# A fused transformer block on one core: the first projection on raw, transposed rows, and four smaller moves

## What is computed

```python
def rmsnorm(x, g):
    y = x * lax.rsqrt(jnp.mean(x * x, axis=-1, keepdims=True) + RMS_EPS)
    return y * g

def hybrid_mixer(h, w_in, ...):                  # h = rmsnorm(x, norm_mix)
    proj = h @ w_in
    (fq, fk, fv, f_logit, nq, kc, vc, ksl, vsl, kwn, vwn,
     nsa_gate_logit, merge_logit) = split_columns(proj, IN_SPLITS)
    ... fox attention on fq, fk, fv; NSA attention on nq with three sets of keys,
    ... rotary turning of nq, ksl, kwn
    g = jax.nn.sigmoid(merge_logit)
    up = jnp.einsum('bsnc,ncd->bsnd', ys, w_branch)
    return jnp.sum(g * up, axis=2) @ w_out

def attention_mixer(h, ...):       # second block: 16 meta tokens ahead of the 256
    ... banded attention with sinks; every query sees the meta tokens too

def deltanet_mixer(h, norm_w, w_in, ...):
    u = rms_norm(h, norm_w) @ w_in
    qkv, z, b, a = jnp.split(u, ...)
    ... causal convolution on qkv, delta rule
    return (rms_norm(o, o_norm_w) * jax.nn.silu(z)) @ w_out

def second_block(x, ...):
    ... return h[:, N_META:]       # the meta rows are dropped at the end
```

## Time and profile before

| | |
|---|---|
| median of 3 runs | 1620.73 us (1619.58 to 1621.23) |
| the profiled execution, its own time | 1621.65 us |
| its span | 1619.6 us |
| TensorE busy | 1584.4 us, 98% of the span |
| VectorE busy | 1164.3 us, 72% |
| ScalarE busy | 904.2 us, 56% |
| GpSimd busy | 105.4 us, 7% |

### The profile page before, as it was taken

The page is one execution under the profiler, slowest core; times in us unless marked ns, Lnnn a source line. Parts: engine busy times, 40 slices in busy tenths (PEclk is TensorE's granted clock), DMA queues, the critical chain, the costliest instruction groups (busy, mean ns, idle before and its releaser), DMA issues. The chain is left out here.

```text
span 1619.6 us, 33683 instructions
## 1 busy us (share of the span) xinstructions
PE 1584.4 (98%) x12906; PEld 1422.1 (88%) x12906; DVE 1164.3 (72%) x1987; ACT 904.2 (56%) x1605; POOL 105.4 (7%) x78
## 2 busy tenths in 40 slices
PE   7999999999999999999999999999999999999998
PEld 6888988999999999998888888878777889988877
DVE  5678666798988999986666666667655658755565
ACT  4357753455556767766666666654565645344443
POOL 0000000200000000000000000006001333200000
PEclk9999999999999999999999999999899999999999
DMA  6642355566555444446666666643233445300014
GB/s 219 185 155 81 114 169 157 170 183 181 182 181 157 143 132 138 131 137 208 194 192 191 192 191 194 194 151 119 65 91 94 152 146 159 128 3 3 3 41 143
DMA packets 63076, 229.56 MB, mean 142 GB/s; under 512 B 7008, under 2 KB 7264, under 8 KB 62960
## 3 DMA queue, kind: packets, MB, share of 16 engines
q1 hardware_dynamic: 62960, 227.94, 45.9%
HBM read 226.86 MB, written 1.05 MB: 141 GB/s over the span
## 5 line engine op out<-in xcount | busy, mean ns | idle before, releaser
L1161 DVE TENSOR_TENSOR tile_low<-weights,tile_high 128x1024 fp32r<-128x1024 f32 x252 | 308.0, 1222 | 131.2 <-ACT tile_high L1151 131.0
L1151 ACT ACTIVATE tile_high<-weights 128x1024 fp32r<-128x1024 f32 x252 | 268.1, 1064 | 134.1 <-issue 134.1
L182 ACT ACTIVATE tile_high<-weights 128x1024 fp32r<-128x1024 f32 x168 | 177.4, 1058 | 213.5 <-issue 58.6
L1233 PE MATMUL banks<-parts,tile_high 128*128 128x256 f32 x2048 | 270.5, 285 | 0.3 <-PEq L3129 0.3
L194 DVE TENSOR_TENSOR tile_low<-weights,tile_high 128x1024 fp32r<-128x1024 f32 x145 | 178.0, 1229 | 122.0 <-ACT tile_high L182 109.7
L1233 PEld LDWEIGHTS banks<-parts,tile_high 128*128 128x128 f32 x2048 | 254.1, 191 | 0.9 <-issue 0.9
L1562 PE MATMUL banks<-tile_high,parts 128*128 128x512 f32 x1024 | 253.0, 389 | 0.9 <-ACT parts L1520 0.9
L1562 PEld LDWEIGHTS banks<-tile_high,parts 128*128 128x128 f32 x1024 | 192.1, 188 | 40.9 <-issue 1.1
L236 PE MATMUL banks<-parts,tile_high 128*128 128x272 f32 (+1 forms) x1136 | 156.8, 290 | 0.8 <-ACT big L323 0.8
L236 PEld LDWEIGHTS banks<-parts,tile_high 128*128 128x128 f32 x1136 | 145.5, 188 | 9.6 <-issue 7.5
L1238 PE MATMUL banks<-parts,tile_low 128*128 128x256 f32 x1024 | 143.7, 283 | 1.0 <-DVE tile_low L1161 1.0
(11 more groups left out here) (417 smaller groups left out, 2221.8 us busy)
## 6 DMA issues: line engine op xcount, KB each, us to landing
weights<-in_peer_u SPq DMA_DIRECT2D x128, 512.0 KB, 3.5
weights<-in_peer_v SPq DMA_DIRECT2D x128, 512.0 KB, 3.5
weights<-in_dn_in SPq DMA_DIRECT2D x49, 512.0 KB, 3.5
weights<-in_in_t SPq DMA_DIRECT2D x19, 512.0 KB, 3.5
weights<-in_attn_t SPq DMA_DIRECT2D x18, 512.0 KB, 3.5
weights<-in_in_m SPq DMA_DIRECT2D x16, 512.0 KB, 3.5
weights<-in_wq SPq DMA_DIRECT2D x16, 512.0 KB, 3.6
weights<-in_dn_out SPq DMA_DIRECT2D x16, 512.0 KB, 3.6
```

Source lines behind the costliest of these rows:

```text
L182: k.nc.scalar.activation(k.high[:, m % 2, :], k.ring.view(n), ACT.Copy).then_inc(*k.high_made.up())
L1151: k.nc.scalar.activation(k.high[:, (s + j) % 2, :], k.ring.buf[:, j % RING, :], ACT.Copy).then_inc(k.high_made.sem, 1)
L1161: k.nc.vector.tensor_tensor(k.low[:, (s + j) % 2, :], k.ring.buf[:, j % RING, :], k.high[:, (s + j) % 2, :].bitcast(F32), ALU.subtract).th ...
L1233: ins = nc.tensor.matmul(ps[:, bank, 0:S], high[:, c, :], x[:, c, :], start=part + c == 0, stop=False)
```

## The change

- **The first projection takes rows that are not normalised.** The host also passes `x` transposed (`xt`). ScalarE and VectorE split `xt * norm_mix` directly; the diagonal matmuls are gone. The root is worked out while the first three tiles run; two matmuls with a matrix of ones then spread its reciprocal over all partitions (`root_row`). Every sum of the projection is multiplied by it on VectorE, the values at their copy, and the 16 merge gates by GpSimd in `attention_stage`. The sigmoid of the gates waits for these.
- **The keys are projected once**: 17 tiles, not 19. VectorE writes the turned keys to both halves of the partitions.
- **In `prepare_stage`** TensorE runs three sixths of the first merge tile ahead of the gates' transposes, not five.
- **The steps of the meta tokens' attention** stand at units 1, 3, 4, 6 and 8; the first two instructions are a step of their own.
- **The `z` tiles** are projected for the 256 tokens alone.

```diff
+def input_projection(k, into, prefetch, following):
...
+        @block.sync
+        def _(sp):
+            sp.dma_start(k.param[:, :], k.dram["param"]).then_inc(*k.param_landed.up(16))
+            for half in range(2):
+                sp.dma_start(columns[:, 4 * half:4 * half + 4, :],
+                             k.dram["xt"][:, 4 * half:4 * half + 4, :]).then_inc(*k.columns_landed[half].up(16))
+            load_tiles(sp, k, 3)
+            for tt in range(NT):
+                sp.dma_start(k.h[:, tt, :], k.dram["x"][:, tt, :]).then_inc(*k.x_landed[tt].up(16))
+            sp.dma_start(k.common[:, :], k.dram["const_common"]).then_inc(*k.common_landed.up(16))
+            load_tiles(sp, k, 10)
...
+        @block.scalar
...
+            for c in range(KC):
+                act.wait_ge(*k.columns_landed[c // 4].at(16))
+                nc.scalar.activation(high[:, c, :], columns[:, c, :], ACT.Copy,
+                                     scale=weight[:, c:c + 1]).then_inc(*parted.up())
+            for n in range(3):
+                make_high(act, k, n)
+            for tt in range(NT):
+                act.wait_ge(*k.x_landed[tt].at(16))
+                nc.scalar.activation(scratch[:, tt, :], k.h[:, tt, :], ACT.Square,
+                                     accum_out=sums[:, tt:tt + 1]).then_inc(*summed.up())
+            act.wait_ge(*chain.at(1))
+            nc.scalar.activation(root, y, ACT.Sqrt).then_inc(*rooted.up())
+            for n in range(3, IN_TILES):
+                make_high(act, k, n)
...
+        @block.vector
...
+            def take(i):
+                dve.wait_ge(k.ring.used.sem, i + 1)
+                sum_halves(k, into(i), ps[:, i % 8, :]).then_inc(*halves.up())
+                dve.wait_ge(*halves.last())
+                nc.vector.tensor_tensor(into(i), into(i), k.root_row, ALU.mult).then_inc(*taken.up())
...
+            for n in range(4, IN_TILES):
+                make_low(dve, k, n)
+                upto = n - 1 if n > 5 else n - 2
+                for i in range(done, upto):
+                    take(i)
+                done = upto
...
+        @block.tensor
+        def _(pe):
+            for i in range(IN_TILES):
+                if i == 3:
+                    pe.wait_ge(*cleared.at(2))
+                    pe.wait_ge(*scaled.at(NT))
+                    for tt in range(NT):
+                        ins = nc.tensor.matmul(ps[:, spread_bank, tt * P:tt * P + P], ones, diagonal(tt),
+                                               start=True, stop=True)
+                    ins.then_inc(*spread.up())
...
+                tile_both(pe, k, i, ps[:, i % 8, :], S, {"left": left} if i == 0 else None)
...
-            merged(0, 0, 5)
+            merged(0, 0, 3)
...
-            swap(NQ)
+            swap(T[:, NQ:NQ + 4, :], 4)
...
-            merged(0, 5, 6)
+            merged(0, 3, 6)
...
-            swap(KSL)
+            swap(k.raw_keys, 2)
...
+        @block.gpsimd
+        def _(pool):
+            for i in range(N_MERGE):
+                pool.wait_ge(gated.sem, i + 1)
+                nc.gpsimd.tensor_tensor(k.T[:, MERGE + i, :], k.T[:, MERGE + i, :], k.root_row,
+                                        ALU.mult).then_inc(*scaled_gates.up())
...
                 if c % 4 == 2:
+                    act.wait_ge(*gates_scaled.at(N_MERGE))
                     part = gate[:, :, 4 * (c // 4):4 * (c // 4) + 4, :]
                     nc.scalar.activation(part, part, ACT.Sigmoid).then_inc(*opened.up())
...
-            meta_steps = (1, 2, 4, 6)
+            meta_steps = (1, 3, 4, 6, 8)
...
-                if u == 1:
+                if u == 2:
                     make_low(dve, k, gate_tile(1))
...
             for u in range(len(units) + 1):
-                if u == 2:
-                    meta["scalar"](act)
                 if u < len(units):
                     exps(u)
+                if u == 3:
+                    meta["scalar"](act)
...
-    psum = lambda kind, i: ps[:, bank[kind](i), 0:L]
+    psum = lambda kind, i: ps[:, bank[kind](i), 0:S if kind == "z" else L]
+    tokens = lambda kind: slice(META if kind == "z" else 0, L)
```

More of the change, by code:

```diff
@@ L323, in merge_gate, with norm_programs @@
     k.nc.scalar.activation(k.T[:, MERGE + i, :], src, ACT.Copy).then_inc(*gated.up())
-def norm_programs(k, tiles, weight, cols, following, halves=True, scaled_rows=False, fetch=()):
+def norm_programs(k, tiles, weight, cols, following, scaled_rows=False, fetch=()):
     nc, ps = k.nc, k.ps
@@ L341, in norm_programs @@
     diagonal = lambda i: scratch[0:tiles[i][1], i, 0:tiles[i][1]]
-    ahead = range(k.tiles[following] + (1 if halves else 0), k.tiles[following] + AHEAD)
+    ahead = range(k.tiles[following] + 1, k.tiles[following] + AHEAD)
     def sync(sp):
-        if not halves:
-            fetch_inputs(sp, k)
         for dst, src in fetch:
@@ L351, in scalar @@
     def scalar(act):
-        if not halves:
-            act.wait_ge(*cleared.at(1))
-            nc.scalar.activation(k.norms[:, 47:48], k.norms[:, 47:48], ACT.Sqrt).then_inc(*loaded.up())
-            for i, (h, rows) in enumerate(tiles):
-                act.wait_ge(*k.x_landed[i].at(16))
-                nc.scalar.activation(scratch[0:rows, i, :], h, ACT.Square,
-                                     accum_out=sums[0:rows, i:i + 1]).then_inc(*summed.up())
-        act.wait_ge(*chain.at(3 if scaled_rows else 2 if halves else 1))
+        act.wait_ge(*chain.at(3 if scaled_rows else 2))
         nc.scalar.activation(root, y, ACT.Sqrt).then_inc(*rooted.up())
@@ L362, in scalar @@
             make_high(act, k, m)
-        if not halves:
-            act.wait_ge(*k.param_landed.at(16))
         for c in range(KC):
@@ L378, in vector @@
         else:
-            if not halves:
-                nc.vector.memset(k.norms[:, 47:48], 1.0).then_inc(*cleared.up())
-            if halves:
-                done(nc.vector.tensor_tensor(sums, sums, k.norms[:, 40:40 + n], ALU.add))
-            else:
-                dve.wait_ge(*summed.at(t))
+            done(nc.vector.tensor_tensor(sums, sums, k.norms[:, 40:40 + n], ALU.add))
             done(nc.vector.tensor_scalar(y, sums, 1.0 / D, EPS, ALU.mult, ALU.add))
@@ L387, in vector @@
         newton(nc, dve, chain, y, root, inv, step)
-        if not halves:
-            dve.wait_ge(*k.common_landed.at(16))
         for i, (h, rows) in enumerate(tiles):
@@ L394, in vector @@
             make_low(dve, k, m)
-        if not halves:
-            dve.wait_ge(*k.param_landed.at(16))
         for c in range(KC):
@@ L406, in product @@
                                     start=True, stop=True)
-        if halves:
-            keep_busy(k, 7, 3)
+        keep_busy(k, 7, 3)
         if t > NT:
@@ L568, in turn_rows, with turn_queries, turn_both_keys @@
         dve.wait_ge(*vec.last())
+    def turn_queries(dve):
+        x, y = T[:, NQ:NQ + 4, :], T[:, KSL:KSL + 4, :]
+        turned_part(dve, 0, x, y, 4)
         nc.vector.tensor_tensor(x, x, y, ALU.add).then_inc(*vec.up())
+        dve.wait_ge(*vec.last())
+    def turn_both_keys(dve):
+        x, y = k.raw_keys, rot[:, 0:2, :]
+        turned_part(dve, 1, x, y, 2)
+        for g in range(2):
+            mine = slice(HD * g, HD * g + HD)
+            for half in range(2):
+                nc.vector.tensor_tensor(T[HD * half:HD * half + HD, KSL + g:KSL + g + 3:2, :], x[mine], y[mine],
+                                        ALU.add).then_inc(*vec.up())
         dve.wait_ge(*vec.last())
@@ L2219, in _ @@
                     pe.wait_ge(*taken.at(i - 1))
-                tile_T(pe, k, first + t, psum(kind, i), lambda c: (high[:, c, :], low[:, c, :]),
+                of = tokens(kind)
+                tile_T(pe, k, first + t, psum(kind, i), lambda c: (high[:, c, of], low[:, c, of]),
                        norm=norm if t == 0 else None)
@@ L3179, in first_block @@
     k.x_landed = k.start("x_landed_0", "x_landed_1")
+    k.columns_landed = k.start("columns_landed_0", "columns_landed_1")
     k.common_landed, k.param_landed, k.const_landed = k.start("common_landed", "param_landed",
                                                                           "const_first_landed")
[L3182 removed]
     with k.joined():
[L3185 to L3187 removed]
+        k.raw_keys = k.rot[:, 2:4, :]
+        into = lambda i: k.raw_keys[:, i - KSL, :] if KSL <= i < KSL + 2 else k.T[:, i if i < KSL else MISC, :]
+        input_projection(k, into, k.tiles["in_fv"] + RING, "in_fv")
         def copy(dst, banks):
```

126 lines of the change are left out of this document (85 added, 41 removed).

## The result

| | before | after |
|---|---|---|
| median, 5 runs of each on one chip | 1621.23 us (1619.58 to 1624.73) | 1608.76 us (1606.69 to 1611.55) |
| ratio of the times | | 0.9922, 95% interval 0.9905 to 0.9938 |
| the profiled execution, its own time | 1621.65 us | 1609.04 us |
| its span | 1619.6 us | 1607.1 us |

In a later comparison, beside other kernels, the changed kernel took 1607.34 us against 1619.45 (ratio 0.9922, 0.9909 to 0.9935). The forecast was 1608.4 us: the sum came out, but not every term of it.

The account below looks back on a forecast made before the run. TensorE, busy 98% of the span, was taken to bound the kernel. The terms sum to -12.3 us; from the profiled 1621.65, less 0.92 to reach the median, this gives 1608.4 us, range 1603.5 to 1615.

Parts of the forecast that it names:

- start: First projection: tile 0 starts at 10.5 us, not 16.06, but at half clock; -2.2 us, between -3.9 and -1.2.
- the root's product per sum: First projection: VectorE's extra 0.43 us multiplication per tile stays hidden under TensorE's 2.82; 0 us.
- keys once: First projection: TensorE runs two tiles fewer; -5.6 us.
- `prepare_stage`: This stage: a 0.8 us wait for the gates' sigmoid against a cheaper keys' permutation; +0.2 us, from -0.9 to +1.1.
- gates on GpSimd: First attention: GpSimd's 13 multiplications hold up VectorE, about 0.1 us a unit reaching TensorE; +1.2 us, from 0 to +4.
- second block's attention: Shifted meta steps remove most of a 1.91 us wait and the half clock behind it; -4.0 us, from -1.6 to -5.3.
- z: Projection of z on 256 tokens, not 272: 16 tiles each 0.12 us shorter; -1.9 us.
- the ring: Weight slots shift with two tiles fewer; sub-keys land at 288.0 us, before their use at 288.73; 0 us, up to +3.
- Rival 1: Second block's attention: the clock still falls, so the part brings only 1.6 us; total 1610.8 us, chance 0.20.
- Rivals 2, 3 and 4: GpSimd's lock reaches TensorE every unit, 1616.3 us (0.10); start brings nothing, 1611.1 (0.10); GpSimd multiplication costs 2.39 us, 1638.3 (0.02).

Follow-up runs that it names:

- the first edit: Changed kernel with the meta tokens' steps back at units 1, 2, 4 and 6 and gate tile 1's split at unit 1: median 1611.89 us.
- the two edits: Changed kernel with the meta tokens' steps at their old places, 1611.89 us; kernel before with only the new places, 1616.76 us against 1621.69.

## Why the prediction was right, point by point

| term | forecast | in the first pair of traces | what the experiments add |
|---|---|---|---|
| start | -2.2 | -2.72 | cold start 1.3 to 2.8, mean 2.1 |
| the root's product per sum | 0 | 0 | |
| keys once | -5.6 | -5.51 | not undone, read from the traces alone |
| `prepare_stage` | +0.2 | +2.40 | +1.3 to +2.4 in five traces, -0.85 without its three waits |
| gates on GpSimd | +1.2 | 0 | 0 with none, under 0.7 with two |
| second block's attention | -4.0 | -5.25 | 5.0 by undoing it, 4.9 by adding it |
| z | -1.9 | -3.24 | 3.25 by undoing it |
| the ring | 0 | 0 | |
| not in the sum: half clock at 1080 us | | +1.62 | in 6 of 12 traces |
| small steps elsewhere | | +0.20 | |
| sum | -12.3 | -12.50 | |

- **Start.** TensorE began at 11.10 and not at 10.5, since the rows landed at 6.80 and not at 5.7; later traces have 9.72 to 10.74, so 10.5 was a fair middle. The half clock cost 1.97 us in tile 0, where I had 2.9 from half of 5.9; the 2.9 is just past the upper end of what nine traces show. The two errors went against each other. The root took the room that I had given it: diagonals at 20.0, tile 2's end at 21.4.
- **`prepare_stage`** is the step that failed, by 2.2 us, and twice the bound of +1.1 that I had given. Five traces have this order and no half clock inside the stage; they take 23.13 to 24.26 us against 21.86, so the error is 1.1 to 2.2. The wait for the sigmoid was 1.43 and not 0.8, since I took the second merge tile's landing, which ScalarE waits for ahead of it, from the trace of before, and it came 0.65 us later against the stage's start. The second wait, 0.44, is this kind of landing again. The third, 1.11, I had denied: "VectorE's work on the keys stays alike (four additions on half the partitions for one on all)". An addition of 64 x 512 takes 0.69 us, as much as one of 128 x 512 (0.68 at L648); the four took 3.33 us, 0.49 of it GpSimd's lock in this one trace, where one of 128 x 1024 had taken 1.23. In these rows the price goes by the columns, not by the partitions. The sum itself was a tenth off: its rows give a wait of 0.8, and I wrote +0.9.
- **Gates.** The mechanism was right, who waits was not: GpSimd for VectorE 0.77 us, VectorE for GpSimd mostly 0.23. And the 9.08 of 10 us busy was one window; over the stage VectorE has a fifth of its time free.
- **Second block's attention.** The mechanism held, and the size within 1 us. TensorE waits at none of the shifted steps, and at most 0.4 us of the +1.0 that I had set against it was spent (1.91 + 3.4 less the 4.95 of the first edit). Of the -5.25, 0.34 is a shorter wait at the stage's end (0.52 for 0.86), which came and went with neither edit. Rival 1 (the clock falls all the same) is refuted for this place by the two edits.
- **z.** The mechanism held, the price of 256 columns was mis-sized: 117.5 ns in this stage, not the 120 of `merge_stage`'s rows, so that a tile brought 0.20 us and not 0.12. The Trainium skill, TensorE: Matmul & The Clock Gate, section "Back-to-back issue gap", has N/2.4 + 2.5 ns for a matmul by itself, by which 16 columns are 6.7 ns and the part -2.6; the rows show 7.5 to 8.3 ns (3.00 and 3.02 against 2.82, over 24), and 3.24 us in all. The page's difference was nearer than the rows that I had picked, its absolute 109 ns was not.
- **Rivals 2, 3 and 4** fell: TensorE lost time to the lock in no unit, the start brought its share in all traces, a multiplication takes 0.64 us alone.

So the total is right because `prepare_stage` and the clock at 1080 us (3.8 us worse together) were paid by four terms that were too careful (4.3 better together). That the errors cancelled is luck: the stretch at 1080 us is in half of the traces of this kernel and its edits, and the four terms depend neither on it nor on `prepare_stage`.

## What to carry to other kernels

When an operation on all partitions becomes several on half of them, count instructions and columns: here each one cost as if it were on all, and the last of them may be the one that the next stage waits for. A wait of an otherwise busy TensorE can be worth more than its length, since a stretch at half clock may follow; the way to know is to undo the one edit and look whether the stretch comes back at the same place. And where TensorE waits for the first data anyway, give it matmuls of ones: they were worth 2 us here.

## What the runs showed of the hardware that I had not expected

- TensorE's clock went to half for 6.8 us in a stretch in which it was busy throughout and had waited for nothing (rows at 82.90 above). Which of the places are hit differs between executions of the same code; why, no run here tells.
- VectorE's instructions with two operands in SBUF were held by GpSimd's even where they are tiny or on half the partitions: one of 4 columns took 0.40 us instead of 0.17, one on 64 partitions 1.18 instead of 0.69. One with a single operand (L992) was held too, 0.55 instead of 0.17, while the reciprocals were not. GpSimd's 0.64 us became 1.41 behind a split. The 2.63 us of the earlier trace rows are the same thing with a longer instruction.
- The first rows landed, by ScalarE's first part with two equal pieces, between 5.4 and 6.8 us in executions of almost the same program, and tile 0's start moved with it.
